# A transformer pair on one core: the first unit of each dense block takes x's high half for all k before the low half, 1/rms moves into the FFN's chunks, and VectorE's queue starts each stage with the residuals

## The reference

```python
def rmsnorm(x, g):
    return x * rsqrt(mean(x * x, axis=-1) + EPS) * g

def swiglu(x, w_in, w_out):                  # w_in 1024 x 5632, w_out 2816 x 1024
    gate, up = split(x @ w_in, 2, axis=-1)
    return (silu(gate) * up) @ w_out

h = first_block(...)                         # ends in rms_norm(xl, g_final)
for i in range(2):
    h = h + 0.5 * swiglu(rmsnorm(h, norm_g[i, 0]), ffn_w_in[i, 0], ffn_w_out[i, 0])
    h = h + (mixer_a, mixer_b)[i](rmsnorm(h, norm_g[i, 1]))
    h = h + 0.5 * swiglu(rmsnorm(h, norm_g[i, 2]), ffn_w_in[i, 1], ffn_w_out[i, 1])
return rmsnorm(h, final_g)
```

## Time and profile before

| what | us |
| --- | --- |
| median of 3 runs | 1946.99 |
| profiled execution | 1944.74 |
| its span | 1943.0 |
| TensorE busy (matmuls) | 1845.9 |
| VectorE busy | 828.1 |
| ScalarE busy | 655.1 |
| GpSimd busy | 166.9 |

### The profile page before, as it was taken

The page is one execution under the profiler, slowest core; times in us unless marked ns, Lnnn a source line. Parts: engine busy times, 40 slices in busy tenths (PEclk is TensorE's granted clock), DMA queues, the critical chain, the costliest instruction groups (busy, mean ns, idle before and its releaser), DMA issues.

```text
span 1943.0 us, 30548 instructions
## 1 busy us (share of the span) xinstructions
PE 1845.9 (95%) x13068; PEld 1542.4 (79%) x13068; DVE 828.1 (43%) x986; ACT 655.1 (34%) x767; POOL 166.9 (9%) x83
## 2 busy tenths in 40 slices
PE   6997789999999998999899999999999999999998
PEld 4973745455454448999898999999998899999998
DVE  4225411111111117444676644474455445575444
ACT  3424210000000015334335543353434355354333
POOL 0110000000000001111001011111110000211110
PEclk8999889999999998999999999999999999999999
DMA  9229559999999994555543355555554444446550
GB/s 345 93 103 368 222 237 421 421 422 421 422 421 422 422 369 159 185 176 181 172 143 109 131 187 182 181 180 181 188 180 131 156 159 164 146 142 204 180 182 34
DMA packets 200216, 444.21 MB, mean 229 GB/s; under 512 B 9175, under 2 KB 157008, under 8 KB 172344
## 3 DMA queue, kind: packets, MB, share of 16 engines
q1 hardware_dynamic: 196928, 437.84, 60.9%
q10 hardware_dynamic: 2776, 2.90, 0.5%
q0 software_dynamic: 416, 2.09, 0.3%
HBM read 441.73 MB, written 1.06 MB: 228 GB/s over the span
## 4 chain that ended last, share of the span: by engine, by line
PE 88%; DVE 6%; ACT 3%; DMA 1%; issue 1%; ACTq 0%; POOL 0%; DVEq 0%
PE wk L680 13%; PE wk L681 13%; PE wk L682 13%; PE wk L1026 11%; PE wk L1046 6%; PE acc L680 6%; PE acc L682 6%; PE acc L681 6%; PE wk L990 3%; PE acc L1006 3%; ACT w_hi L504 1%; DVE con L2112 1%; DVE w_lo L513 1%; PE wk L1258 1%; PE wk L715 1%
## 5 line engine op out<-in xcount | busy, mean ns | idle before, releaser
L513 DVE TENSOR_TENSOR w_lo<-ring,w_hi 128x2048 fp32r<-128x2048 f32 x197 | 450.0, 2287 | 434.2 <-ACT w_hi L504 434.1
L680 PE MATMUL wk<-h_hi,w_hi 128*128 128x256 f32 x1832 | 526.3, 287 | 14.5 <-DVE h_lo L2101 9.5
L504 ACT ACTIVATE w_hi<-ring 128x2048 fp32r<-128x2048 f32 x198 | 377.4, 1907 | 481.0 <-PE wk L682 324.7
L681 PE MATMUL wk<-h_lo,w_hi 128*128 128x256 f32 x1832 | 523.3, 286 | 0.0
L682 PE MATMUL wk<-h_hi,w_lo 128*128 128x256 f32 x1832 | 523.2, 286 | 0.0
L680 PEld LDWEIGHTS wk<-h_hi,w_hi 128*128 128x128 f32 x1832 | 357.2, 195 | 17.5 <-issue 14.7
L681 PEld LDWEIGHTS wk<-h_lo,w_hi 128*128 128x128 f32 x1832 | 357.2, 195 | 0.2
L682 PEld LDWEIGHTS wk<-h_hi,w_lo 128*128 128x128 f32 x1832 | 356.7, 195 | 0.0
L680 PE MATMUL acc<-hid_hi,w_hi 128*128 128x256 f32 x896 | 254.5, 284 | 3.2 <-POOL hid_lo L1779 3.2
L681 PE MATMUL acc<-hid_lo,w_hi 128*128 128x256 f32 x896 | 253.5, 283 | 0.0
L682 PE MATMUL acc<-hid_hi,w_lo 128*128 128x256 f32 x896 | 253.5, 283 | 0.0
(11 more groups left out here) (313 smaller groups left out, 2020.7 us busy)
## 6 DMA issues: line engine op xcount, KB each, us to landing
ring<-in_ffn_w_in_dram SPq DMA_DIRECT2D x88, 1024.0 KB, 5.0
ring<-in_w_gate_dram SPq DMA_DIRECT2D x64, 1024.0 KB, 13.5
ex_ring<-in_w_up_dram SPq DMA_DIRECT2D x64, 1024.0 KB, 16.8
ring<-in_ffn_w_out_dram SPq DMA_DIRECT2D x44, 1024.0 KB, 4.8
ex_ring<-in_w_down_dram SPq DMA_DIRECT2D x32, 1024.0 KB, 13.4
arena<-in_w_down_dram SPq DMA_DIRECT2D x32, 1024.0 KB, 12.5
ring<-in_w_ada_dram SPq DMA_DIRECT2D x24, 1024.0 KB, 7.0
ring<-in_b_w_in_dram SPq DMA_DIRECT2D x24, 1024.0 KB, 5.2
```

The costliest lines, as they stand in the source:

```text
L504: nc.scalar.activation(w_hi[:, v % SPLIT, 0:n], ring[:, u % RING, 0:n], ACT.Copy).then_inc(w_hi_ready, 1)
L513: eng.tensor_tensor(w_lo[:, v % SPLIT, 0:n], ring[:, u % RING, 0:n], w_hi[:, v % SPLIT, 0:n].bitcast(F32), ALU.subtract).then_inc(w_lo_rea ...
L680: mm(dst, w[0], x[0], start=first, stop=False, skip_group_check=True)
L681: mm(dst, w[0], x[1], start=False, stop=False, skip_group_check=True)
```

## The change

1. In a stage's first unit TensorE does the 32 matmuls with `h_hi` for all eight slices, waiting for `h_hi_ready` slice by slice, and then the 16 with `h_lo`, waiting for `h_lo_ready` (`first_project3`; for mixer B `first_rows3`). The number of matmuls is the same.
2. `totals` stands after the second unit, no longer two slices into it.
3. In each FFN chunk VectorE multiplies `sil` by 1/rms a second time, after the silu (a new instruction and a new semaphore, `sil_scaled`). `ffn_resid` is one instruction, x += 0.5 acc, and `y_part` is gone.
4. On VectorE the third of the splits ahead of the residuals moves behind residual 3 (`next_split` of `fold`), except at MoE to F0, where there was none.
5. The squares are added by three `TENSOR_TENSOR` of 1024, 512 and 256 elements a partition (`added`) in place of one `TENSOR_REDUCE`.
6. Mixer B opens three units before the bias rows in place of two, and ScalarE's splits there stand one unit earlier against the GELUs.

```diff
+            def high_terms(dst, w, x, first):
+                mm(dst, w[0], x[0], start=first, stop=False, skip_group_check=True)
+                return mm(dst, w[1], x[0], start=False, stop=False, skip_group_check=True)
+
+            def first_project3(dst, v, fresh):
+                wh, wl = halves(w_hi, v), halves(w_lo, v)
+                for k in range(KT):
+                    pe.wait_ge(h_hi_ready, fresh + k + 1)
+                    for m in range(2):
+                        f = slice(m * P, (m + 1) * P)
+                        high_terms(dst[:, m * T:(m + 1) * T], (wh[:, k, f], wl[:, k, f]), (h_hi[:, k, :],), k == 0 and m == 0)
+                for k in range(KT):
+                    pe.wait_ge(h_lo_ready, fresh + k + 1)
+                    for m in range(2):
+                        last = mm(dst[:, m * T:(m + 1) * T], wh[:, k, m * P:(m + 1) * P], h_lo[:, k, :], start=False,
+                                  stop=k == KT - 1, skip_group_check=True)
+                return last
...
@@ swiglu, TensorE
+                        if ch == 0 and j == 0 and i is None:
+                            last = first_project3(o, v, fresh)
+                        else:
+                            last = project3(o, v)
+                        last.then_inc(unit_done, 1)
                         if ch == 0 and j == 1:
-                            project3(o, v, ks=range(2), closes=False)
                             totals(j_norm, 3)
-                            last = project3(o, v, ks=range(2, KT), opens=False)
...
@@ mixer A, TensorE
+            group(lambda b: first_project3(b, v, 2 * KT), ends_unit=True)
+            aunit(1)
+            totals(1, 3)
...
@@ mixer B, TensorE
-            for a in range(2):
+            for a in range(3):
                 n = g[0]
                 pe.wait_ge(grp_out, n - 3)
-                open_rows(wk[:, n % 4, :], a)
-                if a == 0:
-                    totals(4, (n + 3) % 4)
+                open_rows(wk[:, n % 4, :], a).then_inc(unit_done, 1)
+                if a == 1:
+                    totals(4, (n + 2) % 4)
                 g[0] += 1
...
@@ VectorE
-            def fold(j, gcol, resid):
-                for c in range(4):
-                    resid(c)
-                    if c:
-                        fold_low(j, c - 1, gcol)
+            def added(dst, sq):
+                link(V.tensor_tensor(sq[:, 0:4 * T], sq[:, 0:4 * T], sq[:, 4 * T:8 * T], ALU.add))
+                link(V.tensor_tensor(sq[:, 0:2 * T], sq[:, 0:2 * T], sq[:, 2 * T:4 * T], ALU.add))
+                return V.tensor_tensor(dst, sq[:, 0:T], sq[:, T:2 * T], ALU.add)
+
+            def fold(j, gcol, resid, next_split=None):
+                resid(0)
+                resid(1)
+                fold_low(j, 0, gcol)
+                resid(2)
+                fold_low(j, 1, gcol)
+                resid(3)
+                if next_split is not None:
+                    split_low(next_split)
+                fold_low(j, 2, gcol)
                 fold_low(j, 3, gcol)
                 dve.wait_ge(sq_ready, 4 * (j + 3) + 4)
-                last = V.tensor_reduce(...)
+                last = added(sq_sum[:, T:2 * T] if j == 0 else sq_sum[:, 0:T], scr)
...
@@ hidden, VectorE
                     dve.wait_ge(silu_ready, at(c0 + ch + 1))
+                    V.tensor_tensor(sil[:, ch % 2, :, :], sil[:, ch % 2, :, :], by_rstd(), ALU.mult).then_inc(sil_scaled, 1)
+                    dve.wait_ge(sil_scaled, at(c0 + ch + 1))
...
@@ ffn_resid, VectorE
-                if c >= 2:
-                    dve.wait_ge(resid_ready, (8, 16, 20, 28)[n] + c - 1)
-                link(V.scalar_tensor_tensor(y_part[:, c % 2, :, :], acc[:, m, :], 0.5, by_rstd(), ALU.mult, ALU.mult))
-                V.tensor_tensor(xT[:, m, :], xT[:, m, :], y_part[:, c % 2, :, :], ALU.add).then_inc(resid_ready, 1)
+                V.scalar_tensor_tensor(xT[:, m, :], acc[:, m, :], 0.5, xT[:, m, :], ALU.mult, ALU.add).then_inc(resid_ready, 1)
```

More of the change, by code:

```diff
@@ L702, in project_rows3 @@
                     for k in range(KT):
-                        if fresh is not None and t == 0:
-                            pe.wait_ge(h_lo_ready, fresh + k + 1)
+                        if t == 0:
+                            pe.wait_ge(h_hi_ready, fresh + k + 1)
+                        mm(dst[:, t * UW:(t + 1) * UW], h_hi[:, k, r], wh[:, k, :], start=t == 0 and k == 0, stop=False,
+                           skip_group_check=True)
+                        mm(dst[:, t * UW:(t + 1) * UW], h_hi[:, k, r], wl[:, k, :], start=False, stop=False,
+                           skip_group_check=True)
+                for t in range(TT):
+                    r = slice(t * P, (t + 1) * P)
+                    for k in range(KT):
+                        if t == 0:
+                            pe.wait_ge(h_lo_ready, fresh + k + 1)
+                        last = mm(dst[:, t * UW:(t + 1) * UW], h_lo[:, k, r], wh[:, k, :], start=False, stop=False,
+                                  skip_group_check=True)
+                return last
+            def project_rows3(dst, v, close_row=None, closes=True):
+                wh, wl = halves(w_hi, v), halves(w_lo, v)
+                for t in range(TT):
+                    r = slice(t * P, (t + 1) * P)
+                    for k in range(KT):
                         last = triple(dst[:, t * UW:(t + 1) * UW], (h_hi[:, k, r], h_lo[:, k, r]),
-                                      (wh[:, k, :], wl[:, k, :]), t == 0 and k == 0, not close_row and k == KT - 1)
+                                      (wh[:, k, :], wl[:, k, :]), t == 0 and k == 0, closes and not close_row and k == KT - 1)
                     if close_row:
@@ L1153, in _, with aunit @@
             g0 = 20
-            def aunit(a, rows=False, fresh=None):
+            def aunit(a, rows=False):
                 v = split(U_A + a)
-                group(lambda b: project_rows3(b, v) if rows else project3(b, v, fresh), ends_unit=True)
-            aunit(0, fresh=2 * KT)
-            def second(b):
-                v = split(U_A + 1)
-                project3(b, v, ks=range(2), closes=False)
-                totals(1, 3)
-                return project3(b, v, ks=range(2, KT), opens=False)
-            group(second, ends_unit=True)
+                group(lambda b: project_rows3(b, v) if rows else project3(b, v), ends_unit=True)
+            v = split(U_A)
+            group(lambda b: first_project3(b, v, 2 * KT), ends_unit=True)
+            aunit(1)
+            totals(1, 3)
             def tail(b):
@@ L1278, in _ @@
             pe.wait_ge(binrow_in, 16)
-            for a in range(2):
+            for a in range(3):
                 for t in range(TT):
                     last = close_row(first_banks[a], t, a)
-                last.then_inc(unit_done, 1)
+                last.then_inc(first_closed, 1)
             for j in range(2):
@@ L1287, in _ @@
             last.then_inc(w1_ps, 1)
-            for a in range(2, 12):
+            for a in range(3, 12):
                 v = split(U_B + a)
@@ L2164, in step @@
                     split_low(v + 1 + SPLIT, i)
-                    if ch:
+                    if ch and (i is not None or ch < n - 1 or u0 == U_F[3]):
                         split_low(v + 2 + SPLIT, i)
```

37 lines of the change are left out of this document (19 added, 18 removed).

## The result

The changed kernel takes 1926.89 us (median of 4 runs, 1926.52 to 1929.04) against 1946.84 us (4 runs, 1943.83 to 1949.37): ratio 0.9902, interval 0.9891 to 0.9914. 1926 was predicted. The profiled execution took 1926.52 us with a span of 1924.8. Lines have moved: L514 is the split (was L513), L505 its high half on ScalarE (L504), L681 to L683 the three products (L680 to L682), L780 the sum's matmul in `totals` (L740), L2143 `fold_low` (L2101), L2257 the residual (L2206 and L2207), L2203 `hidden` (L2150), L2196 the new product.

A forecast was written before the change was run, and what follows sets the result against it. TensorE, busy 1845.9 of 1943.0 us, bounds the kernel, so only its pauses and clock can give a gain. Border and end gains of 21.9 us less 1.0 for waits make 20.9, from 1946.99 to 1926 us; range 1920 to 1934.

The forecast's parts named there:

- F1 to F2, 6.0: Border F1 to F2: no wait is left and the clock stays up, so 6.0 us go.
- MoE to F0, 6.4: Border MoE to F0: first unit follows `h_hi`, the sums end sooner, and gate 1 starts 6.4 us earlier.
- F0 to A, 3.6: Border F0 to A: four pauses of TensorE all close, saving 3.6 us.
- A to F1, 0: Border A to F1: TensorE has no such waits there, so nothing to win, 0 us.
- F2 to B, 3.7: Border F2 to B: four pauses worth 4.0 us close except 0.3 us of wait, saving 3.7 us.
- B to F3, 1.5: Border B to F3: two pauses close, saving 1.5 us.
- the third opened unit moves the two bias rows of its own to the others and adds none: Mixer B's head, in the F2 to B term: the number of rows stays the same, so no cost was counted.
- The end, 0.7: End of the kernel: the last residual, one instruction instead of two, is on the path, saving 0.7 us.
- What the waits cost, 1.0: Five fresh units with 16 waits instead of 8: cost between 0 and 3.2 us, taken as 1.0.
- The product and the late `totals`, 0: FFNs: the 44 new products and `totals` 36 matmuls later are covered, at no cost; late `totals` slower as rival, 3%.
- The clock stays low: Rival, 20%: low-clock stretches remain at MoE to F0 and F1 to F2, keeping 6 us: 1932.
- More than the sum: Rival, 8%: one low-clock stretch less, as in mixer A, gives 3 us; with no cost for the waits, 1922.

The follow-up runs named there:

- the five executions above: Changed kernel twice, `reduce`, `product_x3` and `f0_squares`, all with untouched borders at mixer B: 439.5 to 445.4 us from F2's root to F3's, mean 442.6.
- f0_squares: Changed kernel with ScalarE's second-sum squares behind all `h_hi` pairs at MoE to F0, and F0's first unit in its old order of products: 1923.4 us.
- rstd_resid: Changed kernel with 1/rms back as a factor of the residuals (two instructions each) and without the products in the chunks: 1931.7 us.
- product_x3: Changed kernel with two more products of `sil` and 1/rms, never read, ahead of each of the 44: 1927.24 us.
- reduce: Changed kernel with one reduction again in place of the three additions of the squares: 1929.29 us.
- old_order: Changed kernel with each dense block's first unit again doing three products per slice and waiting for `h_lo`: 1931.07 us.

## Why the prediction was right, point by point

The median was right within 0.9 us, and part of that is luck. Between the profiled executions 18.2 us went, not 20.9: against the forecast +0.6 at the first two borders, +0.9 at A to F1, -0.2 at F1 to F2, -5.5 from F2 to F3, -1.0 at the end, +1.0 for the waits (their cost lies within these distances already) and +1.5 of chance at the start. The medians lie 19.95 us apart, since that of the kernel before is 2.1 us above its profiled execution and that of the changed kernel 0.4; these offsets have nothing to do with the working. The two traces of the changed kernel, 16.7 and 22.1 us shorter from the first mark to the last, lie on either side of the 20.9. The waits and the closing of the borders came as worked out; the clock in mixer B didn't.

- *F1 to F2, 6.0*: 5.8. The working held: residual 3 in one instruction at 1273.39, the split behind it, no wait, clock at 1.00. One size was off: `fold_low`'s four instructions took 2.51 us, not 1.67, with GpSimd at work beside the first of them (1274.67 to 1277.24). The cover took it up.
- *MoE to F0, 6.4, and F0 to A, 3.6*: 10.6 together for 10.0. The low stretch behind the 4 us pause stayed; the second one, behind the pause for the sum, is gone.
- *A to F1, 0*: 0.9, which its own spread covers.
- *F2 to B, 3.7, and B to F3, 1.5*: -0.3 in the profiled execution. The waits went as said: there is no row for them. The step that failed is "the third opened unit moves the two bias rows of its own to the others and adds none". It adds no matmul, but it made four rows in a run six, and TensorE at 1.2 GHz followed. I had asked of the clock only whether there was a pause. That is about half of the 5.5 us; the other half is the longer low stretch near 1640 (10 us against 3), at waits that the change doesn't touch. In the mean of the five executions above, 442.6, the two borders gained 2.4; with the run broken up, 3.1 to 4.1. `f0_squares`, which had as little of the low clock there as the kernel before, 3 us, took 439.50 from F2's root to F3's against 445.07: 5.6 us for the 5.2 of the forecast. So the waits were priced rightly, and the clock decides how much of it an execution shows.
- *The end, 0.7*: 0. I took the last residual for the path. The root (L1407 in the marks) waits for TensorE's L774, 16 matmuls of 3.6 us that start as the last down unit ends. They ask for the last square 12 instructions in, at 1930.0 before (an estimate from the first row below), and even then it had been there since 1929.7 (the second). `rstd_resid` has the two instructions back and 182.00 all the same.

```profile
1927.39 3.61 PE L734 MATMUL wk<-scr,con 128*128 128x256 f32 x16
...
1929.04 0.63 ACT L1363 ACTIVATE scr<-xT 128x512 f32<-128x512 f32 x1 [0.81 <-DVE xT L2207]
```

- *What the waits cost, 1.0*: too much. F1-F2 is 190.68 us for 33 units of 5.76, 190.08: at most 0.6 is left for 16 waits and the sum's matmuls. F2's first unit itself took 5.96 us against 5.76: at most 0.2 for its 16 waits, 0.1 for the eight that are new, and 0.6 for six such units. (There are six fresh units, not five, and the bound of 3.2 us counted all 16 waits of each, though eight were there before.)
- *The product and the late `totals`, 0*: right, by `product_x3`, and `totals` has no wait in any FFN. `reduce` shows where cover is thin: 1.9 us at F0's start, where VectorE's splits stand behind the sums.
- *The clock stays low (rival)*: the mechanism was real, the place wrong. Neither F1 to F2 nor the second half of MoE to F0 kept a low stretch; mixer B's head, which no rival named, got one. *More than the sum* had the right source too: where low stretches fall in the mixers moved the executions by more than any other thing.

What stays open is what decides how long a stretch at 1.2 GHz lasts inside the mixers: near 1640 it was 3 to 10 us in kernels with the same code there, and none shows a rule.

## To carry over

Undo the parts of a change one by one and then in pairs: here two parts are worth 4 and 6 us alone and 16 together, in part because at F1 to F2 pauses of 0.5 to 1.3 us left the clock up and pauses of 2.8 us in all did not. Don't make a rule of these lengths: at F2 to B a single 1.9 us (`old_order`) brought a fall, and the 3.0 us in three waits of the kernel before brought none. Mark every block by one instruction that occurs once, and compare distances and not totals: FFN borders could be read to 0.02 us in a kernel whose runs spread over 7 us. Before a column that spreads is read, add up its time at the lower clock, and compare traces that have the same. Look at the granted clock also where TensorE has no pause.
